# A hybrid decoder layer on one core: the place of the weight transposes inside each stick-breaking step

## What is computed

```python
def stick_breaking_attention(q, k, v):
    def block(args):                        # 128 queries at a time
        z = einsum("bhqd,bhkd->bhqk", q_blk, k) * scale
        causal = key_pos[None, :] < q_pos[:, None]
        log_beta = log_sigmoid(z)
        log_keep = where(causal, log_sigmoid(-z), 0.0)
        suffix = cumsum(log_keep, axis=3, reverse=True) - log_keep
        w = where(causal, exp(log_beta + suffix), 0.0)
        return einsum("bhqk,bhkd->bhqd", w, v)
```

## Time and profile before

| | before |
|---|---|
| median of three runs | 2797.88 us |
| the profiled execution's own time | 2801.16 us |
| its span, first to last instruction | 2799.4 us |
| mean granted TensorE clock | 0.982 of full speed |
| TensorE matmul busy | 2674.0 us (96%) |
| VectorE, ScalarE, GpSimd busy | 57%, 39%, 44% |
| stick-breaking stage, about | 363 to 1138 us of the span |

### The profile page before, as it was taken

The page is one execution under the profiler, slowest core; times in us unless marked ns, Lnnn a source line. Parts: engine busy times, 40 slices in busy tenths (PEclk is TensorE's granted clock), DMA queues, the critical chain, the costliest instruction groups (busy, mean ns, idle before and its releaser), DMA issues. The chain is left out here.

```text
span 2799.4 us, 34826 instructions
## 1 busy us (share of the span) xinstructions
PE 2674.0 (96%) x13076; PEld 2238.3 (80%) x13076; DVE 1582.9 (57%) x1770; ACT 1087.5 (39%) x1877; POOL 1225.5 (44%) x732
## 2 busy tenths in 40 slices
PE   6999999999999999799999699999996999999998
PEld 5888878888888888688888577878885888888887
DVE  5100046766677666588877566653369666633343
ACT  4111034444444444466666344442243222232332
POOL 2466634544544544388878633545406222100001
PEclk9999999999999999899999899999998999999999
DMA  3454533343424341466667544434321333364443
GB/s 121 147 173 161 152 99 115 94 124 96 123 91 129 105 128 46 136 190 208 202 198 205 185 166 151 143 135 150 113 110 41 115 118 121 125 230 154 144 158 116
DMA packets 187558, 386.33 MB, mean 138 GB/s; under 512 B 17536, under 2 KB 98048, under 8 KB 187392
## 3 DMA queue, kind: packets, MB, share of 16 engines
q1 hardware_dynamic: 187392, 384.10, 41.8%
HBM read 278.52 MB, written 105.51 MB: 137 GB/s over the span
## 5 line engine op out<-in xcount | busy, mean ns | idle before, releaser
L986 POOL TENSOR_TENSOR sb_beta<-sb_beta,sb_rest 128x128 f32<-128x128 f32 (+7 forms) x128 | 164.2, 1283 | 397.4 <-DVE sb_rest L1046 397.4
L2538 PE MATMUL ff_ps<-ff_mh,ff_total 128*128 128x512 f32 x1024 | 315.7, 389 | 0.4 <-DVE ff_total L2970 0.4
L819 PE MATMUL sb_psg<-uh,sb_wl 128*128 128x512 f32 x768 | 309.9, 404 | 0.0
L819 PE MATMUL sb_psg<-ul,sb_wh 128*128 128x512 f32 x768 | 305.7, 398 | 0.0
L819 PE MATMUL sb_psg<-uh,sb_wh 128*128 128x512 f32 x768 | 304.1, 396 | 0.0
L1046 DVE TENSOR_TENSOR_SCAN sb_rest<-sb_rest 128x128 f32<-128x128 f32 (+7 forms) x128 | 179.6, 1403 | 155.5 <-ACT sb_rest L935 155.1
L1777 PE MATMUL mg_ps<-mg_yh,mg_wh 128*128 128x512 f32 x512 | 207.4, 405 | 28.2 <-DVE mg_yl L1981 27.5
L2538 PEld LDWEIGHTS ff_ps<-ff_mh,ff_total 128*128 128x128 f32 x1024 | 192.2, 188 | 40.9 <-DVE ff_ml L2966 0.8
L1777 PE MATMUL mg_ps<-mg_yl,mg_wh 128*128 128x512 f32 x512 | 201.9, 394 | 0.0
L1777 PE MATMUL mg_ps<-mg_yh,mg_wl 128*128 128x512 f32 x512 | 201.8, 394 | 0.0
L2538 PE MATMUL ff_ps<-ff_ml,ff_total 128*128 128x512 f32 x512 | 199.2, 389 | 0.0
(11 more groups left out here) (327 smaller groups left out, 6988.0 us busy)
## 6 DMA issues: line engine op xcount, KB each, us to landing
ff_w<-in_w_down SPq DMA_DIRECT2D x64, 512.0 KB, 3.5
sb_w<-in_w_in SPq DMA_DIRECT2D x48, 512.0 KB, 4.7
scratch_proj<-sb_out SPq DMA_DIRECT2D x48, 512.0 KB, 2.9
sb_k<-scratch_qk SPq DMA_DIRECT2D x64, 256.0 KB, 6.3
ssd_arow<-scratch_decay SPq DMA_DIRECT2D x32, 512.0 KB, 5.9
mg_w<-in_w_branch SPq DMA_DIRECT2D x32, 512.0 KB, 4.5
mg_raw<-scratch_y SPq DMA_DIRECT2D x32, 512.0 KB, 4.8
mg_gate<-scratch_proj SPq DMA_DIRECT2D x32, 512.0 KB, 3.6
```

Source lines behind the costliest of these rows:

```text
L819: last = nc.tensor.matmul(ps_g[:, h], l[:, s, k], r[:, k, h * HALF:(h + 1) * HALF], start=(k == 0 and j == 0), stop=(k == KB - 1 and j == 2))
L986: nc.gpsimd.tensor_tensor(beta[:, i % 3, 0:cols], beta[:, i % 3, 0:cols], rest[:, i % 3, 0:cols], ALU.mult).then_inc(weighted, 1)
L2538: done = nc.tensor.matmul(acc[:, DOWN_PS[local], cols], l[:, columns(local)], r[:, cols], start=(first and j == 0), stop=(last and j == 2))
```

## The change

In TensorE's loop the fill of a step is no longer cut in two around the transposes. After the scores (and, every fourth step, the product with the values) come the wait for `weighted` and the transposes, and then the whole fill of the step. Step 0, which has no transposes, keeps its order. No instruction is added or taken away, and no other engine's order changes.

```diff
             if i >= Y_LAG and (i - Y_LAG) % 4 == 3:
                 weigh_values(i - Y_LAG)
-            if 0 < i < N:
-                project(fill_from[i], middle)
             if LAG <= i < N + LAG:
                 pe.wait_ge(weighted, i - LAG + 1)
             for u in at_event[i]:
                 turn(u)
             if i < N:
-                project(middle, fill_from[i + 1])
+                project(fill_from[i] if i else middle, fill_from[i + 1])
```

## The result

Over 22 runs each the changed kernel takes 2803.84 us (median; 2796.24 to 2811.51) and the kernel before 2797.73 us. One of the 22 runs before took 11728.36 us, for a reason that is not on record; the other 21 lie between 2792.25 and 2804.25, and the ratio that follows fits those 21 alone. The ratio is 1.0021, with a 95% interval of 1.0013 to 1.0029: 5.9 us slower, somewhere between 3.6 and 8.1. That is inside the 0.3% that I had called no change, though clear of zero, and a third of the 19 us that I forecast. The lower end of my range, 2801, holds the median, but the forecast as I made it, clearly slower by 19 us, was wrong.

The account below looks back on a forecast made before the run. TensorE's own queue was taken to bound the stage. Joining 0, value-step stalls 8.9 and clock falls 10.2 made 19.1 us, on the profiled 2801.16 giving 2820.3, against the median 2817.0 us, 0.7% more; range 2801 to 2830.

Parts of the forecast that it names:

- TensorE's queue sets the stage: Stick-breaking stage: it lasts as long as TensorE's queue, busy 95.02 of 96 us; other engines count only where TensorE waits.
- What joining saves: nothing: Fill of each step: running its two halves together saves 0, since switching between kinds of matmul loses nothing.
- that 0.06 in 127 steps, 7.6 us: Fill behind scores: the most joining could save; taken as 0 because the transposes would bear the same 0.06.
- Transposes wait for nothing new elsewhere: Steps without values: transposes come 1.1 to 2.8 us earlier, yet `weighted` and low parts are ready; cost nothing.
- The value step: +1.1 us each, 8.9: Step 4 of each pair, 8 times: TensorE's stall for the values' low part grows from 1.14 to 2.25 us.
- The clock: 6 falls, +10.2: Behind the value-step stalls: clock falls to half for 3.41 us in 6 of 8 pairs, 1.7 us each.
- The sum: Whole kernel: 0 + 8.9 + 10.2 = 19.1 us slower.
- the second's milder case: Rival: joining saves 7.6 us but the value-step stalls still add 8.9; 2799.2 us, no change; chance 0.05.
- a clock that holds: Rival: only the value-step stalls grow, no clock falls; 2806.8 us; chance 0.20.

Follow-up runs that it names:

- experiment 1: The changed kernel with the eight value steps put back as in the kernel before, fill joined in all other steps; ratio 0.9976 to the kernel before.
- experiments 2 and 8: 2: kernel before with only the eight value steps changed, ratio 1.0037. 8: that kernel traced again, 4 of 8 falls; changed kernel traced twice more, 0 and 1.

## Why the prediction was wrong, point by point

- *TensorE's queue sets the stage.* Right. VectorE's busy time in the 96 us rose from 66.48 to 70.79, ScalarE's fell from 43.09 to 41.64, and outside the value step no wait answered to either.
- *What joining saves: nothing.* This is the step that failed. I had the bound at hand, "the most it could be is that 0.06 in 127 steps, 7.6 us", and argued it away with "that same 0.06 falls on them", on the transposes. They take back only a fifth. In the timelines of the kernel before, between 395 and 1120 us, the first fill matmul behind scores is followed after 0.248 us on average (90 places), behind the values' product after 0.283 (31 places); a settled one after 0.227. I had read one step, whose scores end in a matmul of 128 columns. Behind such a matmul the first distance is 0.282 (61 places), behind a wider one 0.231 (60 places). One of each kind (TensorE, kernel before):

```profile
1031.47 0.27 PE L840 MATMUL sb_psz<-sb_k,sb_q 128*128 128x128 f32 x1
1031.59 0.44 PE L819 MATMUL sb_psg<-uh,sb_wh 128*128 128x512 f32 x1
1031.87 0.40 PE L819 MATMUL sb_psg<-ul,sb_wh 128*128 128x512 f32 x1
...
1035.10 0.34 PE L840 MATMUL sb_psz<-sb_k,sb_q 128*128 128x256 f32 x1
1035.27 0.39 PE L819 MATMUL sb_psg<-uh,sb_wl 128*128 128x512 f32 x1
1035.50 0.40 PE L819 MATMUL sb_psg<-uh,sb_wh 128*128 128x512 f32 x1
```

  The next five fill matmuls are a few nanoseconds slow too, in either kind. When transposes stand there instead, they pay 0.02 to 0.03 us behind a matmul of 128 columns (in the steps with 1, 3, 5 and 7 tiles) and under 0.01 behind a wider one (2, 4, 6 and 8 tiles). Added up over a pair (second to seventh), the stretches of fill take 68.08 us before and 67.14 in experiment 1, 0.94 less, and the transposes 8.62 and 8.81, 0.18 more. That leaves the 0.75: 0.05 a step, 6.0 us over the stage, or 6.6 by the changed kernel's own pair. So the bound held and the choice of 0 did not. Why the first wide matmul behind a narrow one comes late, no run tells.
- *Transposes wait for nothing new elsewhere.* Right: neither `weighted` nor a weights' low part appears in the list but at the stage's end, where it was.
- *The value step: +1.1 us each, 8.9.* Right: +1.05, 8.4 us.
- *The clock: 6 falls, +10.2.* The cost of a fall was right (1.65 measured, 1.7 taken); their number was not, and this is the second step that failed. I counted three of four idle times of that length, at other places of the kernel, as a rate. Three traces of the changed kernel have 1, 0 and 1 of 8. How many falls its 22 timed runs had is not on record. Their mean granted clock is 0.9831, that of all 46 runs of the kernel before beside the experiments 0.9838. The difference of 0.00076 is 2.1 us in 2800, about one fall, and the scatter of the runs leaves about 1 us on it either way; the two sets were not run side by side. The sentence of the Trainium skill that I set beside it (page "TensorE: Matmul & The Clock Gate", "Part 4: PE-mode transpose", transposes don't count as busy as matmuls do) would have had all 8 fall, and these traces speak against that use of it. The advice of the Trainium skill on the length of idle gaps (same page, "Why this matters for your kernels"), by which the clock would hold, fits the changed kernel better, but not the falls behind every second stall in experiments 2 and 8.
- *The sum.* With the measured terms: 8.4 - 6.6 + 2.1 = 3.9 us, at the low end of the measured 3.6 to 8.1. The first two terms are read from traces; the third is an estimate, and whether the rest of the 5.9 us is more falls or something outside the stage stays open. The rival nearest to it was the second's milder case, the saving together with the 8.9, "2799.2, no change", to which I gave 0.05.

The two errors add: 7 us of saving missed and 8 us of clock too many. That 2803.84 still lies inside my range is luck on the first: the range allowed for a clock that holds, but had no saving in it.

## What to carry to other kernels

Where one engine's queue is the bound, work out both signs of a reordering to the hundredth of a microsecond per step, since 127 steps make 6 us of 0.05: a "remainder" in a row is a term, not noise, and one step is too few to read it from. Group narrow matmuls with narrow ones and keep wide ones in one run; move a step forward only where what it waits for isn't queued behind that same step's own work. The change was right in 119 steps and wrong in 8, and an experiment that undoes it in the 8 alone found a version that is faster than both. Spreading the values over two steps, so that no step has three units for two buffers, gave more than either (0.9940).

## What the runs showed of the hardware that I had not expected

- The distance between fill matmuls takes about ten of them to settle. Behind transposes the first is followed after 0.314 us (mean of 121 places of the changed kernel), the second to fourth after 0.232, 0.232 and 0.229, the fifth to ninth after 0.227 to 0.230, and from the tenth on it is 0.227. No run tells why.
- Stalls of 2.0 us cost the clock in every second pair, in two of two traces, when they came about 97 us apart on average (from the third or the first pair on), and in 0 or 1 of 8 in three traces when they came 95.8 us apart. The same length of stall had both outcomes within one trace. The 1.87 us wait at the stage's start was followed by a fall in 7 of the 12 traces that have it.
